# Combining two experts' rows by one product of 128 rows in the MoE stage of a decoder trunk

## The reference

```python
e_idx, gate = route(xf, w_router, b_router)      # best of 8 groups of 4 experts, then 2 experts in it
def expert_block(args):
    xb, e = args
    h = jax.nn.silu(xb @ w_gate[e]) * (xb @ w_up[e])     # 1024 -> 512
    return h @ w_down[e]                                 # 512 -> 1024
y = ...                                          # rows gated and summed over the token's two experts
x = layer_norm(DEEPNORM_ALPHA * x + y, ln_g[l, 2], ln_b[l, 2])
```

## Time and profile before

| | us |
|---|---|
| median of 3 runs | 1109.55 |
| lowest and highest | 1109.03, 1110.74 |
| profiled execution | 1108.49 |
| its span | 1106.7 |
| TensorE busy in the span | 1070.9 |
| VectorE, ScalarE busy | 356.4, 266.7 |

### The profile page before, as it was taken

The page is one execution under the profiler, slowest core; times in us unless marked ns, Lnnn a source line. Parts: engine busy times, 40 slices in busy tenths (PEclk is TensorE's granted clock), DMA queues, the critical chain, the costliest instruction groups (busy, mean ns, idle before and its releaser), DMA issues.

```text
span 1106.7 us, 16406 instructions
## 1 busy us (share of the span) xinstructions
PE 1070.9 (97%) x6806; PEld 551.1 (50%) x6806; DVE 356.4 (32%) x817; ACT 266.7 (24%) x537; POOL 38.3 (3%) x86
## 2 busy tenths in 40 slices
PE   8999999999898999999999999999999999999995
PEld 4444455557655554566544844444444444444442
DVE  0179623234655645203216311212121121202122
ACT  2431122234435520013401111212112121212121
POOL 2000100000000000100000100000000000000000
PEclk9999999999999999999999999999999999999998
DMA  8012320211122150553333899999999999999970
GB/s 277 24 61 76 115 77 2 78 49 49 60 77 84 72 191 1 179 238 120 154 124 119 341 401 422 422 420 421 420 420 406 420 416 417 418 412 421 409 302 9
DMA packets 51229, 252.41 MB, mean 228 GB/s; under 512 B 5329, under 2 KB 6481, under 8 KB 26321
## 3 DMA queue, kind: packets, MB, share of 16 engines
q1 hardware_dynamic: 47616, 246.05, 56.0%
q0 software_dynamic: 2304, 4.20, 1.0%
q10 hardware_dynamic: 1232, 1.07, 0.3%
HBM read 249.21 MB, written 6.29 MB: 231 GB/s over the span
## 4 chain that ended last, share of the span: by engine, by line
PE 53%; issue 4%; DVE 1%; ACT 0%; POOL 0%; POOLq 0%; ACTq 0%; DVEq 0%
PE cpair L1973 19%; PE bank L1983 9%; PE tpair L1996 6%; PE bank L2042 3%; PE bank L1805 2%; PE bank L1785 2%; PE bank L1961 2%; PE tpair L1805 1%; PE bank L1778 1%; PE cpair L1805 1%; PE tpair L1785 1%; PE cpair L1785 1%; PE cpair L1887 1%; PE tpair L1827 1%; PE bank L2020 1%
## 5 line engine op out<-in xcount | busy, mean ns | idle before, releaser
L1973 PE MATMUL cpair<-ring,xgT 128*64 128x512 f32 x496 | 130.7, 592 | 0.0
L2398 DVE COPY hT<-bank 128x256 f32<-128x256 f32 x32 | 13.6, 425 | 330.2 <-PE bank L1962 330.2
L1973 PEld LDWEIGHTS cpair<-ring,xgT 128*64 128x64 f32 x496 | 41.8, 137 | 70.4 <-issue 70.3
L1996 PEld LDWEIGHTS tpair<-sel,xgt 128*128 128x128 f32 x256 | 60.9, 328 | 10.7 <-issue 10.6
L2198 ACT ACTIVATE hs<-cpair 64x512 f32<-64x512 f32 x32 | 18.9, 589 | 188.8 <-PE cpair L1973 188.8
L1996 PE MATMUL tpair<-sel,xgt 128*128 128x128 f32 x256 | 64.0, 404 | 0.0
L922 PE MATMUL bank<-xT,ring 128*128 128x512 f32 x128 | 60.9, 606 | 0.0
L365 PE MATMUL bank<-xT,ring 128*128 128x512 f32 x112 | 48.5, 593 | 0.0
L1983 PE MATMUL bank<-ring,hT 128*64 128x512 f32 x208 | 47.8, 598 | 0.0
L2204 ACT ACTIVATE ye<-bank 128x512 f32<-128x512 f32 x32 | 19.0, 593 | 111.9 <-PE bank L1983 111.9
L2042 PE MATMUL bank<-ye,combT 64*128 64x512 f32 x128 | 41.7, 629 | 0.7 <-ACT ye L2204 0.7
(11 more groups left out here) (425 smaller groups left out, 1759.0 us busy)
## 6 DMA issues: line engine op xcount, KB each, us to landing
ring<-in_w_exp_gate SPq DMA_DIRECT2D x31, 1024.0 KB, 9.9
ring<-in_w_exp_up SPq DMA_DIRECT2D x31, 1024.0 KB, 9.9
ring<-in_w_exp_down SPq DMA_DIRECT2D x26, 1024.0 KB, 9.9
ring<-in_w_in SPq DMA_DIRECT2D x6, 2048.0 KB, 8.1
ring<-in_w_mem_kv SPq DMA_DIRECT2D x4, 2048.0 KB, 10.0
xT<-in_w_exp_down SPq DMA_DIRECT2D x7, 1024.0 KB, 10.8
avq<-in_w_exp_down SPq DMA_DIRECT2D x7, 1024.0 KB, 9.8
mixT<-in_w_exp_gate SPq DMA_DIRECT2D x6, 1024.0 KB, 11.2
```

Of the source, the lines that this page charges most:

```text
L1973: last = nc.tensor.matmul(bank[b][m * CAP:(m + 1) * CAP, :], x(h, j), w(m, h)[:, j * DE:(j + 1) * DE], start=(k == 0), stop=(k == KT - 1))
L1996: last = nc.tensor.matmul(tpair[:, h, k * P:(k + 1) * P], xgt[:, g % 2, h * 512 + k:(h + 1) * 512:KT // 2], sel[:, :, :].rearrange("p e c ...
```

## The change

The placing matrices of two experts of a pair stand side by side in one selg of 128 columns, in a single buffer. It is written and turned twice for each pair: for even n with the even expert on the left, for odd n with the two exchanged, which gives combT 0 and combT 1. down puts the column halves of odd experts into exchanged partitions of bank 5. ScalarE copies bank 5 by halves, so that ye 0 holds the first 512 columns of both experts of the pair, one in each half of the partitions, and ye 1 the other 512. combined(p) then is two products of 128 rows for each pair, in odd rounds and behind the last down. The semaphores' counts follow. For the last expert VectorE copies one of the two halves of bank 5. The order of each engine's rounds is as before.

```diff
--- before.py
+++ after.py
@@ -1521,7 +1521,7 @@
         hT = sb("hT", [P, 2, FT, CAP])
         ye = sb("ye", [P, 2, DE])
         sel = sb("sel", [P, 2, CAP])
-        selg = sb("selg", [P, 2, P])
+        selg = sb("selg", [P, P])
         combT = sb("combT", [P, 2, P])
         ln3_here, xg_here = sem("ln3_here"), [sem(f"xg_here{s}") for s in range(2)]
         sel_done, selg_done = sem("sel_done"), sem("selg_done")
@@ -1975,12 +1975,12 @@
                                                         start=(k == 0), stop=(k == KT - 1))
                         return last
 
-                    def down_terms(ht, w, h):
+                    def down_terms(ht, w, h, odd=0):
                         for j in range(FT // 2):
                             k = h * FT // 2 + j
                             for m in both:
                                 o = j * D + m * 512
-                                last = nc.tensor.matmul(bank[5][m * CAP:(m + 1) * CAP, :], ht[:, k, :],
+                                last = nc.tensor.matmul(bank[5][half[m ^ odd], :], ht[:, k, :],
                                                         w(2, h)[:, o:o + 512], start=(k == 0), stop=(k == FT - 1))
                         return last
 
@@ -2013,34 +2013,34 @@
                             pe.wait_ge(ht_read, e)
                         turned_hidden(hb).then_inc(ht_full, 1)
 
-                    def placing_turned(e):
-                        pe.wait_ge(selg_done, e + 1)
-                        if e:
-                            pe.wait_ge(comb_read, e)
-                        nc.tensor.transpose(bank[4][:, 256 + e % 2 * P:256 + (e % 2 + 1) * P], selg[:, e % 2, :], ident[:, :])\
+                    def placing_turned(n):
+                        pe.wait_ge(selg_done, 2 * n + 2)
+                        if n:
+                            pe.wait_ge(comb_read, n)
+                        nc.tensor.transpose(bank[4][:, 256:256 + P], selg[:, :], ident[:, :])\
                             .then_inc(comb_full, 1)
 
                     def down(e):
                         pe.wait_ge(ht_read, e + 1)
                         if e:
-                            pe.wait_ge(y_read, e)
+                            pe.wait_ge(y_read, 2 * e)
                         else:
                             pe.wait_ge(more_known, 1)
                         for h in range(2):
                             piece_here(pe, number[e, 2, h])
-                            last = down_terms(hT[:, e % 2, :, :], lambda i, h: piece(e, i, h), h)
+                            last = down_terms(hT[:, e % 2, :, :], lambda i, h: piece(e, i, h), h, e % 2)
                             last.then_inc(w_read, 1)
 
-                    def combined(e):
-
-                        i, g = e % EPG, e // EPG
-                        pe.wait_ge(y_read, e + 1)
-                        pe.wait_ge(comb_read, e + 1)
+                    def combined(p):
+                        i, g = p % 2, p // 2
+                        pe.wait_ge(y_read, 4 * p + 4)
+                        pe.wait_ge(comb_read, 2 * p + 2)
                         if i == 0 and g:
                             pe.wait_ge(square_done, 2 * g)
                         for h in range(2):
-                            last = nc.tensor.matmul(bank[6 + h][:, :], combT[half[h], e % 2, :], ye[half[h], e % 2, :],
-                                                    start=(i == 0), stop=(i == EPG - 1))
+                            last = nc.tensor.matmul(bank[6 + h][:, :], combT[:, h, :], ye[:, h, :],
+                                                    start=(i == 0), stop=(i == 1))
                         last.then_inc(c_done, 1)
 
                     chosen(0)
@@ -2050,17 +2050,16 @@
                         if e:
                             placing_turned(e - 1)
                             hidden(e - 1)
-                        if e >= 2:
-                            combined(e - 2)
+                        if e % 2 and e >= 3:
+                            combined(e // 2 - 1)
                         if e % 2 and e < LAST:
                             chosen((e + 1) // 2)
                         if e:
                             down(e - 1)
                     placing_turned(LAST)
                     hidden(LAST)
-                    combined(LAST - 1)
                     down(LAST)
-                    combined(LAST)
+                    combined(pairs - 1)
 
                     def body(blk):
                         pe.wait_ge(f_hit, blk)
@@ -2200,8 +2199,10 @@
                     def rows_read(e):
                         act.wait_ge(w_read, read_at[e, DN, 1])
                         if e >= 2:
-                            act.wait_ge(c_done, e - 1)
-                        nc.scalar.activation(ye[:, e % 2, :], bank[5][:, :], ACT.Copy).then_inc(y_read, 1)
+                            act.wait_ge(c_done, e // 2)
+                        for h in range(1 if e == LAST else 2):
+                            s = half[h ^ e % 2]
+                            nc.scalar.activation(ye[s, h, :], bank[5][s, :], ACT.Copy).then_inc(y_read, 1)
 
                     def deviation(g):
                         act.wait_ge(mean_done, g + 1)
@@ -2386,11 +2387,14 @@
                             V.tensor_scalar(sel[:, e % 2, :], caps[:, 0:CAP], table[:, 0, e:e + 1], None, ALU.is_equal)\
                                 .then_inc(sel_done, 1)
 
-                    def placing(e):
-                        if e >= 2:
-                            dve.wait_ge(comb_full, e - 1)
-                        V.tensor_scalar(selg[:, e % 2, :], caps[:, :], table[:, 0, e:e + 1], table[:, 1, e:e + 1],
-                                        ALU.is_equal, ALU.mult).then_inc(selg_done, 1)
+                    def placing(n):
+                        if n:
+                            dve.wait_ge(comb_full, n)
+                        for s in range(2):
+                            e = n // 2 * 2 + (s ^ n % 2)
+                            V.tensor_scalar(selg[:, s * CAP:(s + 1) * CAP], caps[:, 0:CAP], table[:, 0, e:e + 1],
+                                            table[:, 1, e:e + 1], ALU.is_equal, ALU.mult).then_inc(selg_done, 1)
 
                     def turned(e):
                         dve.wait_ge(ht_full, e + 1)
@@ -2398,10 +2402,15 @@
                         V.tensor_copy(hT[:, e % 2, :, :].rearrange("p k c -> p (k c)"), bank[4][:, 0:FT * CAP])\
                             .then_inc(ht_read, 1)
 
-                    def placing_turned(e):
-                        if e >= 2:
-                            dve.wait_ge(c_done, e - 1)
-                        V.tensor_copy(combT[:, e % 2, :], bank[4][:, 256 + e % 2 * P:256 + (e % 2 + 1) * P]).then_inc(comb_read, 1)
+                    def placing_turned(n):
+                        if n >= 2:
+                            dve.wait_ge(c_done, n // 2)
+                        V.tensor_copy(combT[:, n % 2, :], bank[4][:, 256:256 + P]).then_inc(comb_read, 1)
+                    def rows_read():
+                        s = half[1 ^ LAST % 2]
+                        dve.wait_ge(w_read, read_at[LAST, DN, 1])
+                        V.tensor_copy(ye[s, 1, :], bank[5][s, :]).then_inc(y_read, 1)
 
                     def hidden(e):
                         dve.wait_ge(sil_done, e + 1)
@@ -2411,7 +2420,7 @@
 
                     def finished(g):
                         x = xgt[:, g % 2, :]
-                        dve.wait_ge(c_done, EPG * (g + 1))
+                        dve.wait_ge(c_done, 2 * (g + 1))
                         dve.wait_ge(xg_here[g % 2], 16 * (g // 2 + 1))
                         for h in range(2):
                             v = x[:, h * 512:(h + 1) * 512]
@@ -2446,6 +2455,7 @@
                             finished(e // EPG - 1)
                     turned(LAST)
                     placing_turned(LAST)
+                    rows_read()
                     finished(NGRP - 1)
 
                     def body(blk):
```

## The result

The changed kernel takes 1175.3 us (median, 1174.9 to 1175.4) against 1109.4 (with a fourth run, 1109.19, added to the three above): a ratio of 1.059, 95% interval 1.057 to 1.061, **slower by 66 us**. Its profiled execution took 1175.35 us with a span of 1173.6. The forecast was 1168, range 1154 to 1188.

What follows compares the result with a forecast made beforehand. TensorE was taken as the bound, the weight stream running ahead. 1108.5 + 12.2 (products) - 2.7 (even rounds) + 39.3 (single buffer) + 0.6 (tail) + 7.0 (clock) + 2.5 (gather) = 1167.4; forecast 1168 us, range 1154 to 1188.

Steps and rivals of the forecast that it cites:

- The bound: Expert stage: TensorE sets the pace, the weight stream runs ahead, and a microsecond between two products is one of the kernel.
- The single buffer: Seven even rounds: finished, queued behind the waiting placing, delays the hT copy and down; +5.61 against 2.12, +39.3 us in all.
- The two half placings: VectorE after the turning of the placing matrix: two half-width placings need about 0.41 us.
- the chain of 6.56: VectorE's finished(g) with ScalarE free, ahead of the hidden copy in stalled rounds: 6.56 us long.
- The products: Combining in 15 odd rounds: four full instructions take 1.72 us of path instead of 0.91; +12.2 us.
- The even rounds: Eight plain even rounds without combining: down starts 0.34 us earlier, the hT copy being uncovered; -2.7 us.
- The clock: Down after each of seven idle stretches of TensorE: slower by 1.0 us (bounds 0 and 3.43); +7.0 us.
- The gather: Chosen in round 4g+7 waits for group g+2's transfer: one late arrival, +2.5 us, bounds 0 and 15.
- Rival (a): Every group's gather is late for chosen: 12.5 us more, 1180 us; chance 0.10.
- The tail: Kernel's end: down(31) starts 0.34 earlier, bank copies 0.05 later, then four full instructions 0.86 more; +0.6 us.
- The signs: Expected in the profile: seven L1983 waits of about 6 us, unbroken finished, PE busy about 1065, PE digits 7-8, DMA below 9.
- (b): The clock stays at 1.2 GHz over all of each down after a stall: 1185 us; chance 0.06.

Runs made afterwards that it cites:

- the last experiment: The kernel before, with chosen moved ahead of hidden in seven odd rounds (3, 7, ... 27); measured 1109.4 us, ratio 1.000.

## Why the prediction was right

The mechanism was right and the sum came within 8 us of the profiled time; of its terms the clock was sized at less than half of what it cost.

**The bound.** Right: every microsecond put between TensorE's products came out in the span, and outside the stalls only round 23 waited for a transfer. One reading was loose: the slices in which both digits are 9 are 15, not the last 16. Nothing hangs on it.

**The single buffer**: right in mechanism and place, confirmed from both sides (taking it out of the changed kernel, putting it alone into the one before). Forecast +39.3, measured +40.6. The two half placings took 0.54 us, not the 0.41 of the row I had taken them from (one with a single scalar operand); the chain of 6.56 was exact. The gate_up in between is 7.0 us, not 6.9, which no term uses.

**The products**: forecast +12.2, measured +10.5 (8.8, 1.3 and 1.0 in the table, less 0.6 of round 23, which are the gather's). I had missed two things that partly cancel: four instructions held the path for 1.82 and not 1.72, and chosen behind them is 0.22 shorter than behind products of 64 rows. The Trainium skill (TensorEngine Tiling, Key Properties) says that changing the tiling mode drains TensorE; the 0.22 us, which stays away in round 7 of the last experiment, would fit, though no run shows a drain as such. The even rounds gave back 0.33 of the 0.91, which is what was forecast (0.34).

**The clock** is the term that was mis-sized, though right in kind. Forecast 1.0 us a stall, measured 2.2, midway between the 1.0 and the upper bound of 3.43. I had taken it from the one short drop of the earlier trace rows. That drop lasted 3.4 us, from 650.0 to 653.4, and its first 1.5 us fell on chosen, which a low clock hardly lengthens, so that only the rest was paid in down. After a real idle stretch the clock was low from before the first product of down, for 56% of down or more. The experiment with a busy TensorE shows that in the stalls idleness is the cause. The Trainium skill (TensorE: Matmul & The Clock Gate, What's actually happening) says so too: throttled is the default state, and activity releases it.

**The gather**: forecast 2.5 us, measured at most 0.6 (round 23, where it lands at 1015.64, chosen starts 0.38 late and takes 0.2 more). The weight queue did catch up: its waits for TensorE rose from 10.0 and 8.6 on two lines to 86.1 and 111.1 us, and from the issue of a scatter to that of its gather it took 5.0 to 6.3 us and not the 8.6 of the earlier trace rows. But the stream did not run dry in the stall, as I had thought: its share is 1.01 in six of the seven stalls (in the last, with all weights loaded, 0.00) and falls only behind them, to between 0.59 and 0.83 beside down in these six. Rival (a) was close all the same: take 2.2 us of slow products away and three of six gathers are late. Here one loss hid another.

**The tail**: +0.6 forecast, +0.7 measured. What no step had is the +2.1 us ahead of round 1, in a part that the change does not touch. It is a drop of the granted clock near 457 us (mean 0.72 from 455 to 460) that the profile of before does not have. The eight profiles of this study bear it out. T0 of round 1 is 646.3 or 646.4 in the two without a drop between 15 us and that point, 648.0 to 648.3 in the four with one (near 304 or near 457), and 649.3 with both. The eighth, at 649.7, has the one near 457 and another at 11 us. Such drops come and go with the changed part untouched, so the +2.1 is scatter and not an effect of the change.

**The signs.** The wait at L1983, the single run of finished and the PE digits came as forecast. Two signs did not: PE's busy time rose to 1086.7 us and did not fall to 1065, since the slow products after the stalls count as busy, and the DMA digits stayed at 9, as the shares above explain. With (a) and (b) both true the sum would have been about 1197 us, outside the range given.

The terms missed by +1.3 (the buffer), -1.7 (the products), +8.2 (the clock), -1.9 (the gather) and +2.1 (ahead of round 1); the sum of them, some 8 us, is as large as the clock's alone only because the other four cancel, which is luck.

## What to carry to other kernels

Before a buffer is shared or dropped, read what is queued behind the instruction that will wait for it: the wait was free here, a normalisation of 6.6 us behind it was not, and issuing that normalisation ahead of the wait would have saved 58 us. Two products of 64 rows that run side by side already cost what one of 128 rows does, so merging them saves no time, and a short step may be worth its place only for the copy that it hides. Price an idle stretch of TensorE with the slow products after it, here more than a third as much again, and look at which products these are: down's paid for the low clock in full, chosen's hardly.

## What was not expected of the hardware

- The drop after an idle stretch of some 6.6 us cost between 1.3 and 2.8 us in the next products, and a drop can also come with TensorE busy. The eight profiles have twelve such drops in the expert stage, and all twelve begin while chosen runs, two of them behind a late gather; what sets them off was not tested.
- Sixteen instructions of 128x128 behind a product of 128 rows take 3.70 us to the next work, behind products of 64 rows 3.93. With a mean granted clock of 0.57 to 0.60 over them they take 3.93 to 4.03 there.
- Useless products in a stall made a kernel faster by 10 us.
